# Six distances between the matmul operands of one kernel, modulo 256 bytes

## The reference, cut to what matters

```
hybrid layer (twice):
    proj = x @ w_in                      # 1024 -> 3608 columns
    short convolution, delta rule (4 heads), gated linear attention (4 heads), gated norms
    y = o @ w_out ;  x = layer_norm(ALPHA * x + y)
second block, layer 0: stick-breaking attention;  layer 1: dilated attention
    m = attention(rms_norm(x) @ w_qkv) @ w_o ;  x = x + rms_norm(m)
    h = rms_norm(x) @ w_up               # 1024 -> 5632
    h = causal conv of 3 taps + bias ;  f = (silu(h[:2816]) * h[2816:]) @ w_down
    x = x + rms_norm(f)
```

## Time and profile before

| | |
|---|---|
| median of 3 runs | 2085.93 us (2083.0 to 2086.07) |
| profiled execution, its own time | 2079.45 us |
| its span, first to last instruction | 2077.7 us |
| mean granted clock of TensorE | 0.985 |
| TensorE busy | 1980.7 us, 95% of the span |
| weight loads (LDWEIGHTS) busy | 1573.5 us, 76% |
| VectorE, ScalarE, GpSimd busy | 1158.4, 850.1, 309.7 us |
| matmuls | 11438 |

### The profile page before, as it was taken

The page is one execution under the profiler, slowest core; times in us unless marked ns, Lnnn a source line. Parts: engine busy times, 40 slices in busy tenths (PEclk is TensorE's granted clock), DMA queues, the critical chain, the costliest instruction groups (busy, mean ns, idle before and its releaser), DMA issues. The chain is left out here.

```text
span 2077.7 us, 27850 instructions
## 1 busy us (share of the span) xinstructions
PE 1980.7 (95%) x11438; PEld 1573.5 (76%) x11438; DVE 1158.4 (56%) x1454; ACT 850.1 (41%) x1212; POOL 309.7 (15%) x258
## 2 busy tenths in 40 slices
PE   8999899899988989898999999999999999999998
PEld 5677896577777768655778888886788878888886
DVE  4446556654656553276478547735563557745753
ACT  4236433523643351265354324424345444423432
POOL 0200523120051320044220000022000012000002
PEclk9999999999999999999999999999999999999999
DMA  6111103221110222210232232233221203232321
GB/s 237 64 67 53 42 2 122 101 80 63 41 43 34 89 93 90 95 37 1 81 101 95 85 107 89 83 110 125 98 82 61 76 28 110 80 104 102 102 84 69
DMA packets 30786, 167.70 MB, mean 81 GB/s; under 512 B 2827, under 2 KB 9635, under 8 KB 14916
## 3 DMA queue, kind: packets, MB, share of 16 engines
q1 hardware_dynamic: 30228, 165.13, 22.7%
q10 hardware_dynamic: 432, 0.79, 0.1%
HBM read 159.58 MB, written 10.00 MB: 82 GB/s over the span
## 5 line engine op out<-in xcount | busy, mean ns | idle before, releaser
L313 PE MATMUL psum<-inputs_high,weights_high 128*128 128x512 f32 x928 | 384.9, 415 | 17.3 <-DVE inputs_low L261 9.4
L315 PE MATMUL psum<-inputs_high,weights_low 128*128 128x512 f32 x928 | 366.7, 395 | 0.0
L314 PE MATMUL psum<-inputs_low,weights_high 128*128 128x512 f32 x928 | 366.6, 395 | 0.0
L2180 PE MATMUL psum<-inputs_high,weights_high 128*128 128x512 f32 x704 | 276.2, 392 | 0.5 <-DVE inputs_low L2324 0.5
L2181 PE MATMUL psum<-inputs_low,weights_high 128*128 128x512 f32 x704 | 274.0, 389 | 0.0
L2182 PE MATMUL psum<-inputs_high,weights_low 128*128 128x512 f32 x704 | 274.0, 389 | 0.0
L266 DVE TENSOR_TENSOR weights_low<-weights_raw,weights_high 128x2048 fp32r<-128x2048 f32 x66 | 154.7, 2343 | 162.0 <-ACT weights_high L255 162.0
L313 PEld LDWEIGHTS psum<-inputs_high,weights_high 128*128 128x128 f32 x928 | 175.6, 189 | 76.8 <-DVE inputs_low L261 13.8
L314 PEld LDWEIGHTS psum<-inputs_low,weights_high 128*128 128x128 f32 x928 | 176.0, 190 | 41.2 <-issue 5.7
L315 PEld LDWEIGHTS psum<-inputs_high,weights_low 128*128 128x128 f32 x928 | 175.7, 189 | 40.5
L255 ACT CAST weights_high<-weights_raw 128x2048 fp32r<-128x2048 f32 x66 | 125.3, 1899 | 153.6 <-PE psum L315 137.8
(11 more groups left out here) (403 smaller groups left out, 3168.8 us busy)
## 6 DMA issues: line engine op xcount, KB each, us to landing
weights_raw<-w_stream SPq DMA_DIRECT2D x116, 1024.0 KB, 4.8
weights_raw<-w_down SPq DMA_DIRECT2D x32, 704.0 KB, 4.1
residual_parked<-residual SPq DMA_DIRECT2D x2, 2048.0 KB, 10.7
residual_back<-residual_parked SPq DMA_DIRECT2D x2, 2048.0 KB, 7.7
residual<-x_t SPq DMA_DIRECT2D x2, 1024.0 KB, 9.9
bias_by_row<-bias_rows SPq DMA_DIRECT2D x2, 1024.0 KB
bias_by_row<-bias_rows SPq DMA_DIRECT2D x1, 1536.0 KB
out_t<-residual SPq DMA_DIRECT2D x5, 256.0 KB, 2.0
```

The costliest lines, as they stand in the source:

```text
L313: pe.matmul(out, hi, self.ahi[:, k], start=start and b == 0, stop=False)
L314: pe.matmul(out, hi, self.alo[:, k], start=False, stop=False)
L315: mm = pe.matmul(out, lo, self.ahi[:, k], start=False, stop=stop and b == blocks - 1)
L2180: pe.matmul(out, wh, hi, start=start, stop=False)
```

## The change

A function `spacer` allocates a buffer of a given number of bytes per partition that nothing uses, and `operands` allocates one ahead of the inputs where it is given a size. Six calls get a size, two of them another one in each layer. The feed-forward stage has a second spacer between its inputs and its hidden tensors.

```diff
+def spacer(nc, stack, size):
+
+    stack.enter_context(sbuf(nc, "spacer", [P, size // 4], F32))
...
-def operands(nc, k, inputs):
+def operands(nc, k, inputs, later=0):
     with ExitStack() as stack:
+        if later:
+            spacer(nc, stack, later)
         k.ahi = stack.enter_context(sbuf(nc, "inputs_high", [P, inputs, T], F32R))
...
 # hybrid_projections
-    with operands(nc, k, KD), ExitStack() as stack, phase(
+    with operands(nc, k, KD, (64, 128)[layer]), ExitStack() as stack, phase(
 # norms_and_output
+    with operands(nc, k, KD, (128, 192)[layer]), ...
 # output_product
+    with operands(nc, k, KD, 128), ...
 # stick_projections
+    with operands(nc, k, KD, 160), ...
 # feed_forward
+    with operands(nc, k, KD, (32, 96)[layer]), ...
+        spacer(nc, stack, (32, 64)[layer])
         hhi, hlo = sb("hidden_high", [P, DOWN_BLOCKS, T], F32R), sb("hidden_low", [P, DOWN_BLOCKS, T], F32R)
```

More of the change, by code:

```diff
@@ L1383, in norms_and_output @@
     steps = [(c, kk) for kk in range(together) for c in range(2)] + [(c, kk) for c in range(2) for kk in range(together, KD)]
-    with operands(nc, k, KD), ExitStack() as stack, phase(
+    with operands(nc, k, KD, (128, 192)[layer]), ExitStack() as stack, phase(
             nc, *GEMM, "residual", "square_sum", "inv_ln", "inv_norm", "spread", "gained", "gated", "first_sum", "middle_sum", "middle", "shifted", "left_over", "centred", "square",
@@ L1591, in output_product @@
     chunks, per, banks = OUT_CHUNKS, 2, 4
-    with operands(nc, k, KD), ExitStack() as stack, phase(
+    with operands(nc, k, KD, 128), ExitStack() as stack, phase(
             nc, *GEMM, "square", "added", "out_sum", "inv_ln", "inv_out", "next_high", "next_low", landed=k.landed) as s:
@@ L1767, in gain @@
         return k.second[:, C_GAIN + j:C_GAIN + j + 1]
-    with operands(nc, k, KD), ExitStack() as stack, phase(
+    with operands(nc, k, KD, 160), ExitStack() as stack, phase(
             nc, *GEMM, "v_freed", "left_over", "scaled_x", "new_x", "square", "added", "x_sum", "inv_ln", "inv_norm", "turned", "column", landed=k.landed) as s:
@@ L2116, in gain @@
         return k.second[:, at:at + 1]
-    with operands(nc, k, KD), ExitStack() as stack, phase(
+    with operands(nc, k, KD, (32, 96)[layer]), ExitStack() as stack, phase(
             nc, "split", "high", "made", "freed", "in_hi", "in_lo", "x_sum", "x_ln", "inv_x", "scaled",
```

## The result

The changed kernel takes 2110.13 us (median of 4 runs, 2106.06 to 2114.82) against 2086.0 for the kernel before (2083.0 to 2087.19). The ratio is 1.0111, with a 95% interval of 1.0093 to 1.013: 24.1 us slower. 2112 was forecast. The profiled execution has a span of 2108.4 us.

What follows compares the result with a forecast made beforehand. TensorE, busy 1980.7 of 2077.7 us, was taken to bound the kernel. Feed-forward +21.1, stick +3.8 and output +1.3 made +26.2 us on 2085.9, so 2112 us (own range 2107 to 2116; overall range 2090 to 2122).

Steps and rivals of the forecast that it cites:

- The frame: Whole kernel: TensorE bounds it; each stage changes by its matmuls times new price minus old, all on the path.
- Distance 32 = 233.3: Matmuls put at distance 32: 233.3 ns each, read from six swapped matmuls in `token_block` taking 1.40 us.
- the mirror argument: Unseen distances: reversing the sign of moving minus stationary keeps the price, since +32 and -32 both cost 233.3 ns.
- Distance 64 = 233.3, by mirror of 192: Matmuls put at distance 64: 233.3 ns each, as -64 (192) costs in `norms_and_output`.
- 96, 128, 160 = 233.3: Distances that no row had: taken at 233.3 ns, between ends of 215 and 236.7.
- The rival with cheap states there: Some of 96, 128, 160 at 226.7 ns: 2100 us with 96 and 160, 2091 with all three; chance 0.27.
- the one without any stall: Unknown distances at 215 ns: 2053 us for all 3216 matmuls, 2079 if only 96; chance 0.09.
- 236.7 at a multiple of 32 bytes: Rival, worse than anything seen: 96, 128 and 160 at 236.7 ns, total +36.9, 2123 us; chance 0.09.
- not the distance: Rival: another trait of the hybrid stages makes them dear, so all stays at 2086 us; chance 0.09.
- Feed-forward +21.1: Both feed-forward layers: 3168 matmuls go from 226.7 to 233.3 ns, 21.1 us more.
- The sum: Feed-forward, stick and `output_product` terms together: +26.2 us, hybrid and dilated stages adding nothing.
- The base: Starting time for the sum: run median 2085.9 us, giving 2112; the profiled 2079.45 would give 2105.7.

Runs made afterwards that it cites:

- micro: Separate kernel of bare 128x512 split-product streams, computing nothing of the reference, with operand distances shifted in steps of 4 bytes; 226.7 ns at distance 0, up to 240.0.
- zero: Kernel before, with spacers of 32 and 64 bytes in the hybrid stages only, so all stages lie at distance 0; 2079.32 us, ratio 0.9971.
- noff: Changed kernel without the feed-forward spacers, all others kept; 2089.11 us, ratio 1.0013 against the kernel before.
- shifted: Changed kernel with 32 bytes more ahead of weights_high, so addresses move and every distance stays; 2113.79 us in one run.
- ff160: Kernel before, with inputs and hidden of both feed-forward layers put at distance 160; 2106.99 us, ratio 1.009.

## Why the prediction was right

- *The frame* (TensorE bounds, a stage changes by its count times the change of price) was right. 3936 matmuls left distance 0, and nothing else paid: the other engines' work is 0.4% longer at most and hidden.
- *Distance 32 = 233.3*, from the swapped tiles: 233.3, but the reading did not carry it. Those six matmuls come right behind an interruption, and the earlier trace rows has 232 ns in that place at distance 0 too. So rows 8 could not tell distance 32 from 0, and "+32 and -32 agree", on which the mirror argument rests, had not been seen. That 32 does cost 233.3 was luck; micro and the feed-forward layer show it. In `zero` the same six matmuls, now at distance 0, take 1.39 us where rows 8 have 1.40:

```profile
65.68 0.39 PE L339 MATMUL psum<-weights_high,inputs_low 128*128 128x512 f32 x1
...
67.07 0.39 PE L339 MATMUL psum<-weights_high,inputs_low 128*128 128x512 f32 x1
```

- *Distance 64 = 233.3, by mirror of 192*: wrong. It is 228.9. 32 and 224 do cost the same, but no rule stands behind it: reversing the sign changes 64 to 192 (228.9 and 233.3) and 96 to 160 (233.3 and 234.3), as micro shows with shifted weights. This cost 720 matmuls (528 hidden, 192 in `norms_and_output`) x 4.4 ns = 3.2 us of the sum.
- *96, 128, 160 = 233.3*: 233.3, 232.4 to 233.3, and 234.3. The guess from the unsettled states was within 1 ns, and it was a guess: the finer distances of micro run from 228.7 to 240.0, so nothing in the rows of before kept 96, 128 and 160 near 233.3. That 160 is 1 ns dearer adds 0.9 us on 912 matmuls; that 128 is up to 0.9 cheaper takes off 0.3 on 384. The rival with cheap states there and the one without any stall are out; so are 236.7 at a multiple of 32 bytes and "not the distance".
- *Feed-forward +21.1*: the prices make 19.3, the stretches 17.7. The rest is the head of each stretch, where a wait hides a dearer matmul; I had counted every matmul as on the path. Stick +3.8: 3.6. Output +1.3: 1.1. Hybrid 0: -0.8 in the two output products.
- *The sum*: with the measured prices it is 23.6 us and not 26.2, and the stages above grew by 21.5. The medians differ by 24.1, with about 4 us of interval to either side, so the 2 us between 2112 and 2110.13 are less than the measurement tells and no proof of the terms.
- *The base*: I added the sum to the median of the runs and not to the profiled execution, and gave no cause for the 6.5 us between them. Most of it is the granted clock in hybrid layer 1, as the windows above show. From the profiled time the sum would have given 2105.7; the profiled execution of the changed kernel took 2110.11.
- The Trainium skill's rule that the weight load takes nothing from the running matmul (TensorE: Matmul & The Clock Gate, "Step-by-step: what each phase is for") cannot be kept for `float32r`: micro has prices from 226.7 to 240.0 ns with nothing but the distance of the two operands changed, and from 226.7 to 234.2 when only the place of the weights is. For 16-bit operands the trace agrees with it, and with that page's 215.7 ns ("Wait — 56ns, not 53.3ns?"): 215.8.

## What to carry to other kernels

Read the price of a matmul from start to start, stage by stage: two prices for the same line and shape are a finding, even at 95% busy. For `float32r` matmuls of 128x512 put moving and stationary operand at the same address modulo 256 bytes; a stray 32-byte tensor between them costs 3%, and a misplacement by 4 bytes costs 5%. For other numbers of columns the cheapest distance can be another, as the tables above show. Do not read a price from the first matmuls after an interruption, where 0 and 32 look alike. And do not extend a price by symmetry to a case that no row has: a kernel of bare streams settles all of them in one run.

## What the runs showed of the hardware that was not expected

- A dense `float32r` stream settles into a cycle of start-to-start times. The four streams of 504 matmuls kept their price to the end. At distance 0 all times are 226 to 227 ns; at 20, 68, 100, 116 and 196 bytes all are 240 once settled. At 192 they alternate between 231 and 236 in the kernel before and are all 233 to 234 in micro, with the same mean of 233.3: the distance sets the mean here, while the single times differ.
- With fewer stationary columns the prices do not fall towards 215, so the length of the weight load does not set the excess. With fewer moving columns the excess falls, from a mean of 18.6 ns at 512 to 11.0 at 256. What meets at what moment was not resolved.
- Distance 128 settled at 232.4 in the changed kernel, at 233.3 in `noff`, and at both in `shifted`: what came before the stream may matter, and no run varies that alone.
- In `noff`, `ff160`, `shifted` and `zero` the first eight or so matmuls of `output_product` start 427 ns apart (granted clock 0.60 over 3 us there in `ff160`), which costs 1.6 us: 45.3 us at distance 0 in `ff160` and `zero`, 43.6 in the kernel before. A stage time is compared only after a look at its head.
- The stretch of 1460 small matmuls in hybrid layer 1 took 95 us in one profile and 100 to 101 in the six others, with the granted clock at 0.98 against about 0.90. That is 0.25% of the kernel, as much as the 0.3% that distance 0 gained.
